# Building the first expert block's token list on chip while routing, gathering its rows in the projection's stage, and issuing that stage's last stores from ScalarE

## The chip, the core and the metric

The kernel runs on one core of a Trainium2 chip. A core has five engines with programs of their own: TensorE (PE, the matrix products), VectorE (DVE), ScalarE (ACT), GpSimd (POOL) and SyncE (SP, which here only issues transfers). They share an on-chip memory of 128 partitions and wait for each other by semaphores. The metric is the device time of one execution in microseconds, compared by the median of several runs.

## What is computed

One layer of a decoder: an input projection, two groups of attention heads (differential, and sliding window with sinks), an output projection with residual, a router that gives each of the 2048 tokens two of 32 experts, the experts, and a last norm.

```python
def reference(x, norm1_g, w_in, ..., w_gate, w_up, w_down, final_g):
    for l in range(L):                                   # L = 1
        n1 = rms_norm(x, norm1_g[l])
        qkv = n1 @ w_in[l]                               # 2048x1024 @ 1024x2304
...
        o_diff = diff_attention(dq, dk, dv, lam, subln_g[l], lambda_init)
        o_swa = swa_sink_attention(sq, sk, sv, sinks[l])
        x = x + jnp.concatenate([o_diff, o_swa], axis=-1) @ w_out[l]
        n2 = rms_norm(x, norm2_g[l])
        x = x + hier_moe(n2, ...)
    return rms_norm(x, final_g)

def hier_moe(xn, w_rg, b_rg, w_re, b_re, w_gate, w_up, w_down):
...
    p_top, g_idx = lax.top_k(pg, 1)                      # one of 4 groups
    v2, i2 = lax.top_k(el_sel, TOP_K_IN_GROUP)           # 2 of the 8 experts in it
    gates = jax.nn.softmax(v2, axis=-1) * p_top
    expert_id = (g_idx * EXPERTS_PER_GROUP + i2).astype(jnp.int32)
...
    def run_block(args):
        xb, e = args
        h = jax.nn.silu(xb @ w_gate[e]) * (xb @ w_up[e]) # 1024 -> 512
        return h @ w_down[e]                             # 512 -> 1024
```

An expert gets its tokens in blocks; the order of the tokens in a block is free.

## The kernel before

The program is a row of stages, each a block at whose end all engines meet at a barrier: `projection` (0 to about 545 us), `diff_attention` (to 790), `window_attention` (to 1061), `output_projection` (to 1329), `experts` (to 2231) and `combine` (to 2277). Products that need fp32 accuracy are made of three products of high and low parts (lines 62 to 64).

**`output_projection`** walks over 16 tiles of 128 tokens. Its order is written out by hand, engine by engine, and each engine does what stands in its program in that order. For tile t:

- TensorE does the first half of `project(t)`, then `turn(t-1)` (transposing the normed rows `n2` of the tile before), the second half of `project(t)`, `turn_o(t+1)`, then `count(t-2)` (ranks of the tokens within their experts, by a triangular matrix, line 1456) and `route(t-1)` (the router's logits, line 1449). `count` waits until VectorE has done the first step of the `place` before it.
- VectorE does `residual(t)` (h = projection + x, line 1142), `low_o(t+1)`, `normalize(t)` (n2, line 1150), `sub_norm(t+2)` (onorm, four instructions, line 1158), `low_swa(t+2)`, for tiles 1 to 8 the low part of an early weight piece (`low_w`, line 1176), then `choose(t-1)` (group and experts, 16 small instructions, lines 1185 to 1212) and `place(t-2)` (lines 1220 to 1242). `place` works out `dest`, the slot of each of a token's two choices, and `pair`, what is put there: the token's number and its gate. After the last tile `block_table` works out from the counts where each expert's blocks start and end.
- ScalarE squares `o_raw` and `h`, copies the high parts and the turned tiles, and does the exponentials of the gates.
- GpSimd takes the roots and scatters the pairs of tile t-3 into `slots_scratch` in HBM (line 1386, two indirect transfers a tile). Its program ends with a wait for all scatters.
- SyncE waits for `h` of tile t, stores it (line 1532), and only then issues the loads `swaT` and `o_raw` for tile t+2 (lines 1495, 1497), stores `n2` (line 1538) and loads x for tile t+2. At the last tile it first issues six weight loads of 1 MB each for the experts (`FIRST_LOADS`), then the last stores of `h` and `n2`, and waits for all stores.

In HBM, slot d = LISTED * p + b is place p of block b, where `LISTED` is 512, so that the first block of expert 0 holds the slots 0, 512, 1024 and so on. The slots were filled before with the number of an empty token.

**`experts`** goes over 32 experts in 47 blocks of 128 slots. GpSimd loads all slots back (line 1730), copies from them the 128 token numbers of the first block (`fetch`, line 1706) and gathers their rows of `n2` from HBM into `x` (line 1710); for later blocks it does so one block ahead. TensorE meanwhile runs 40 warming transposes (`spin`, line 56), then `turn_x(0)` (line 1836), 16 more of them, and then the products of the block (24 each for gate, up and down). ScalarE and VectorE split each tile and weight into high and low parts.

Of the kernel before, what the change touches and what calls it, by code (L numbers as in the profile page):

```python
# [7 lines left out]
F32 = mybir.dt.float32  # L8
# [1001 lines left out]
def output_projection(nc, sem, x, o_d, mix_d, wo_hi, wo_lo, wo_raw, wo_split, subln_g, norm2_g, w_rg, b_rg, w_re, b_re,  # L1010
                      ident, power, tables_d, n2_d, acc_d, slots_d, starts, ends, w_d, wg, wu,
                      hi_ready, lo_ready, next_raw, raw_in):
# [9 lines left out]
    with ExitStack() as ctx:  # L1022
# [28 lines left out]
        tri_f = sb("tri_f", [P, P])  # L1051
        consts = sb("consts5", [P, 3, E])
# [39 lines left out]
        spare = proj[:, 0, 1, 0:P]  # L1092
        count_ps = proj[0:E, 1, 1, 0:1]
# [39 lines left out]
        PLACE = 9  # L1133
        PLACED = TILES * PLACE

        with nc.Block() as block:
            @block.vector
            def _(dve):
# [105 lines left out]

                def block_table():
# [7 lines left out]
                    dve.wait_ge(counted, TILES + 2)  # L1253
                    dve.tensor_copy(start_row[:, :], start_ps).then_inc(place_step, 1)
# [14 lines left out]
                for t in range(TILES):  # L1269
# [4 lines left out]
                    if t == 0:  # L1274
                        dve.wait_ge(table_in, 32)
                        dve.tensor_copy(tri[:, :], tri_f[:, :])
                        dve.memset(ones[:, :], 1.0)
                        dve.memset(before[:, :, :], 0.0)
# [13 lines left out]
                    if t >= 2:  # L1292
                        place(t - 2, s)
                place(LAST - 1, 1 - LAST % 2)
                choose(LAST, LAST % 2)
                place(LAST, LAST % 2)
                block_table()

            @block.scalar
            def _(act):  # L1300
# [46 lines left out]
                for t in range(TILES):  # L1347
# [23 lines left out]
            @block.gpsimd  # L1371
            def _(pool):

                def sub_root(t, s):
                    pool.wait_ge(oss_ready, t * DK + DK)
                    pool.tensor_tensor(ovar[:, s, :], oss[:, s, :], power[:, 1:2].to_broadcast([P, DK]), ALU.add)\
                        .then_inc(ovar_ready, 1)
                    pool.wait_ge(ovar_ready, t + 1)
                    pool.tensor_tensor(orstd[:, s, :], ovar[:, s, :], power[:, 0:1].to_broadcast([P, DK]), ALU.pow)\
                        .then_inc(orstd_ready, 1)  # L1380

                def scatter(t):
                    pool.wait_ge(place_step, (t + 1) * PLACE)
                    pool.wait_ge(placed, 1)
                    for k in range(TOPK):
                        pool.indirect_dma_start(slots_d, bass.IndirectOffsetOnAxis(ap=dest[:, t, k:k + 1], axis=0),
                                                pair[:, t, k, :], None).then_inc(scattered, 16)

                sub_root(0, 0)
                sub_root(1, 1)  # L1390
                pool.wait_ge(tables_ready, 1)
                for k in range(TOPK):
                    ins = pool.tensor_copy(pair[:, :, k, 0].bitcast(I32), tok_i[:, :])
                ins.then_inc(placed, 1)
                for t in range(TILES):
                    s = t % 2
                    pool.wait_ge(ss_ready, t + 1)
                    pool.tensor_tensor(var[:, s:s + 1], ss[:, s:s + 1], power[:, 1:2], ALU.add).then_inc(var_ready, 1)
                    pool.wait_ge(var_ready, t + 1)
                    pool.tensor_tensor(rstd[:, s:s + 1], var[:, s:s + 1], power[:, 0:1], ALU.pow)\  # L1400
                        .then_inc(rstd_ready, 1)
                    if t + 2 < TILES:
                        sub_root(t + 2, s)
                    if t >= 3:
                        scatter(t - 3)
                for t in range(LAST - 2, TILES):
                    scatter(t)
# [666 lines left out]
```

## Time and profile before

| | |
|---|---|
| median of 3 runs | 2275.84 us (2271.41 to 2279.14) |
| the profiled execution | 2278.96 us, of which span 2277.1 us |
| busy over the span | TensorE 2086.3 us (92%), VectorE 1315.0 (58%), ScalarE 1116.1 (49%), GpSimd 514.0 (23%) |
| 1061 to 1329.5 us (output projection) | TensorE 243.8 of 268.5 us, VectorE 145.4 |
| 1329.5 to 2231 us (experts) | TensorE 876.2 of 901.5 us, VectorE 568.3 |
| mean granted clock of TensorE | 0.96 |

Busy time is the time in which an engine had an instruction under way. Waits between engines say more about what sets the pace: a view of them names, for each idle stretch, the instruction that ended it. Times in the rows below are from the start of the span; "SPq" and "POOLq" are the issues of transfers.

### The profile page before, as it was taken

What the parts mean: (1) busy time and instruction counts of PE and PEld (TensorE: products, weight loads), DVE (VectorE), ACT (ScalarE), POOL (GpSimd) and SP (SyncE); (2) the same over time, 40 slices, a digit from 0 to 9 for tenths busy, and PEclk for the clock granted to TensorE, in tenths of its full rate; (3) what the DMA queues carried; (4) which work ended last, traced back from release to release, by engine and by line L of the source; (5) the groups of instructions that cost most, each with busy time, mean ns of one, the idle gap of its engine ahead of it and who ended that gap; (6) DMA issues with size and microseconds to landing.
All of it is one profiled execution on the core that took longest, in us unless ns stands there. A gap on an engine that the chain in (4) does not pass through costs nothing. (4 is left out here: it accounts for less than half of the span.)

```text
span 2277.1 us, 39542 instructions
## 1 busy us (share of the span) xinstructions
PE 2086.3 (92%) x12823; PEld 1775.3 (78%) x12824; DVE 1315.0 (58%) x2425; ACT 1116.1 (49%) x2395; POOL 514.0 (23%) x624
## 2 busy tenths in 40 slices
PE   6999999979999994998999969999999999999990
PEld 5888888857777773997888858788888888888880
DVE  5333333348888881663555549656666648666533
ACT  4111111138778881663342337556656547666443
POOL 1111111114443434100132221111121111111114
PEclk9999999979999997998999979999999999999995
DMA  7333333252312108332554369978888979998828
GB/s 209 95 99 103 99 94 94 83 156 82 89 56 84 58 12 193 90 93 84 176 185 140 124 228 360 362 213 280 286 276 287 297 217 329 314 322 256 271 46 313
DMA packets 299719, 407.46 MB, mean 179 GB/s; under 512 B 17249, under 2 KB 211553, under 8 KB 299617
## 3 DMA queue, kind: packets, MB, share of 16 engines
q1 hardware_dynamic: 279952, 349.76, 46.1%
q0 software_dynamic: 16176, 55.09, 10.3%
q10 hardware_dynamic: 3504, 1.51, 0.3%
q8 instruction: 47, 0.77, 0.1%
q14 instruction: 40, 0.32, 0.1%
HBM read 314.01 MB, written 92.83 MB: 179 GB/s over the span
## 5 line engine op out<-in xcount | busy, mean ns | idle before, releaser
L62 PE MATMUL proj<-w_in_lo,n1T_hi 128*128 128x512 f32 (+1 forms) x640 | 245.8, 384 | 13.1 <-DVE w_in_lo L260 13.1
L63 PE MATMUL proj<-w_in_hi,n1T_lo 128*128 128x512 f32 (+1 forms) x640 | 240.3, 375 | 0.0
L64 PE MATMUL proj<-w_in_hi,n1T_hi 128*128 128x512 f32 (+1 forms) x640 | 240.0, 375 | 0.0
L534 ACT ACTIVATE prob<-score,nmax 128x512 f32<-128x512 f32 (+3 forms) x344 | 207.3, 612 | 37.0 <-DVE nmax L620 33.4
L62 PE MATMUL u_ps<-wu_lo,xT_hi 128*128 128x256 f32 x752 | 209.8, 279 | 0.0
L64 PE MATMUL u_ps<-wu_hi,xT_hi 128*128 128x256 f32 x752 | 209.7, 279 | 0.0
L63 PE MATMUL u_ps<-wu_hi,xT_lo 128*128 128x256 f32 x752 | 209.6, 279 | 0.0
L1789 DVE TENSOR_TENSOR wg_lo<-raw_pieces,wg_hi 128x1024 fp32r<-128x1024 f32 x124 | 149.0, 1221 | 91.8 <-ACT wg_hi L1761 90.0
L573 POOL TENSOR_SCALAR prob<-prob,scale,lam 128x512 f32<-128x512 f32 (+3 forms) x172 | 147.3, 867 | 229.5 <-DVE scale L636 212.9
L620 DVE TENSOR_REDUCE nmax<-score 128x2 f32<-128x1024 f32 (+3 forms) x172 | 171.3, 996 | 16.3 <-PE score L664 9.0
L62 PE MATMUL y_ps<-wd_lo,hT_hi 128*128 128x512 f32 x376 | 154.6, 411 | 5.2 <-DVE hT_lo L1800 4.5
L682 PE MATMUL o_ps<-v_sb,aT 128*128 128x128 f32 x1088 | 153.3, 279 | 5.6 <-ACT o_diff L561 4.3
L1789 DVE TENSOR_TENSOR wd_lo<-raw_pieces,wd_hi 128x1024 fp32r<-128x1024 f32 x128 | 148.3, 1219 | 13.4 <-ACT wd_hi L1781 10.8
L62 PEld LDWEIGHTS proj<-w_in_lo,n1T_hi 128*128 128x128 f32 x640 | 121.8, 190 | 36.6 <-DVE w_in_lo L260 9.4
L63 PE MATMUL y_ps<-wd_hi,hT_lo 128*128 128x512 f32 x376 | 149.8, 398 | 0.0
L64 PE MATMUL y_ps<-wd_hi,hT_hi 128*128 128x512 f32 x376 | 149.6, 398 | 0.0
L62 PE MATMUL g_ps<-wg_lo,xT_hi 128*128 128x512 f32 x376 | 149.0, 396 | 0.0
L63 PE MATMUL g_ps<-wg_hi,xT_lo 128*128 128x512 f32 x376 | 148.7, 395 | 0.0
L64 PE MATMUL g_ps<-wg_hi,xT_hi 128*128 128x512 f32 x376 | 148.7, 395 | 0.0
L1717 POOL DMA_INDIRECT acc_scratch<-y,own x48 | 84.6, 1763 | 282.2 <-issue 271.0
L682 PEld LDWEIGHTS o_ps<-v_sb,aT 128*128 128x128 f32 x1088 | 136.6, 193 | 11.2 <-ACT o_diff L561 10.8
L63 PEld LDWEIGHTS u_ps<-wu_hi,xT_lo 128*128 128x128 f32 x752 | 142.8, 190 | 2.1
(244 smaller groups left out, 5022.0 us busy)
## 6 DMA issues: line engine op xcount, KB each, us to landing
raw_pieces<-in_w_down SPq DMA_DIRECT2D x64, 1024.0 KB, 10.1
raw_pieces<-in_w_gate SPq DMA_DIRECT2D x62, 1024.0 KB, 9.6
raw_pieces<-in_w_up SPq DMA_DIRECT2D x62, 1024.0 KB, 10.3
qk_scratch<-qkT SPq DMA_DIRECT2D x96, 256.0 KB, 2.3
x_sb<-in_x SPq DMA_DIRECT2D x16, 512.0 KB, 4.2
h<-in_x SPq DMA_DIRECT2D x16, 512.0 KB, 5.5
acc_scratch<-h SPq DMA_DIRECT2D x16, 512.0 KB, 3.0
n_scratch<-n SPq DMA_DIRECT2D x16, 512.0 KB, 4.6
```

What stands on the lines that cost most here:

```text
L62: pe.matmul(out, hi, w_lo, start=first, stop=False)
L63: pe.matmul(out, lo, w_hi, start=False, stop=False)
L64: return pe.matmul(out, hi, w_hi, start=False, stop=last)
L534: act.activation(prob[:, n % RING, c, 0:w], score[:, n % BUFS, c, 0:w], ACT.Exp, bias=nmax[:, c, n:n + 1], accum_out=part[:, c, n:n + 1]). ...
L573: pool.tensor_scalar(prob[:, u % RING, 1, 0:w], prob[:, u % RING, 1, 0:w], scale[:, 1, u:u + 1], lam[:, 5:6], ALU.mult, ALU.mult).then_inc ...
L620: dve.tensor_reduce(nmax[:, :, n:n + 1], score[:, n % BUFS, :, 0:w], AX.X, ALU.max, negate=True).then_inc(max_ready, 1)
L682: mm = pe.matmul(o_ps[:, :], aT[:, u % 2, b * P:(b + 1) * P], v[:, h, j // P + b, :], start=(u == FIRST[m] and b == 0), stop=(u == LAST[m] ...
L1717: pool.indirect_dma_start(acc_d, bass.IndirectOffsetOnAxis(ap=own[:, 0:1].bitcast(I32), axis=0), y[:, :], None, compute_op=ALU.add).then_i ...
L1789: dve.tensor_tensor(piece(LO, k), raw_piece(raw, k), piece(HI, k), ALU.subtract)\
```

## The change

During routing, VectorE writes after each `place` also the list of the tokens of expert 0's first block. The new step `enlist(t)` compares the slots 0, 512, 1024 ... (`row0`, a constant table laid out along the free axis) with the two destinations of each token of the tile, multiplies by the token's number, and adds the result to `listed` (128x128, f32). After the last tile TensorE sums `listed` over the partitions by a product with a column of ones, VectorE writes that as `fetch`, and GpSimd gathers the rows into `x` still in this stage, after the stores of `n2` have landed and before it waits for its scatters. In `experts` the first gather goes away; `x` and `fetch` are now allocated outside of it. The last stores of `h` and `n2` are issued by ScalarE and no longer by SyncE behind its six weight loads.

```diff
@@ output_projection, @block.vector
+                def enlist(t):
+                    base = t * PLACE + 9
+                    dve.wait_ge(place_step, t * PLACE + 6)
+                    dve.tensor_copy(dest_f[:, :], dest[:, t, :]).then_inc(place_step, 1)
+                    dve.wait_ge(place_step, base + 1)
+                    for k in range(TOPK):
+                        dve.scalar_tensor_tensor(out=hit[:, k, :], in0=row0[:, :], scalar=dest_f[:, k:k + 1],
+                                                 in1=consts[:, 2, t:t + 1].to_broadcast([P, P]),
+                                                 op0=ALU.is_equal, op1=ALU.mult).then_inc(place_step, 1)
+                    for k in range(TOPK):
+                        dve.wait_ge(place_step, base + 3 + k)
+                        dve.tensor_tensor(listed[:, :], listed[:, :], hit[:, k, :], ALU.add).then_inc(place_step, 1)
+                    dve.wait_ge(place_step, base + 5)
...
-        PLACE = 9
+        PLACE = 14
...
                     dve.wait_ge(counted, TILES + 2)
+                    dve.tensor_scalar(fetch[:, :], listed_ps, 0.0, None, ALU.add).then_inc(fetch_ready, 1)
+                    dve.wait_ge(counted, TILES + 3)
                     dve.tensor_copy(start_row[:, :], start_ps).then_inc(place_step, 1)
...
                     if t >= 2:
                         place(t - 2, s)
+                        enlist(t - 2)
                 place(LAST - 1, 1 - LAST % 2)
+                enlist(LAST - 1)
                 choose(LAST, LAST % 2)
                 place(LAST, LAST % 2)
+                enlist(LAST)
                 block_table()
@@ @block.scalar
                     if t >= 2:
                         gate_exps(t - 2, s)
+                    if t == LAST:
+                        act.dma_start(acc_d[t * P:(t + 1) * P, :], h[:, s, :]).then_inc(h_stored[s], 16)
+                act.wait_ge(n2_ready, TILES)
+                act.dma_start(n2_d[LAST * P:TILES * P, :], n2[:, LAST % 2, :]).then_inc(stored[LAST % 2], 16)
                 turned_n2(LAST, LAST % 2)
@@ @block.tensor
+                pe.wait_ge(place_step, PLACED)
+                pe.matmul(listed_ps, listed[:, :], ones_f[:, 0:1], start=True, stop=True).then_inc(counted, 1)
@@ @block.gpsimd
                 for t in range(LAST - 2, TILES):
                     scatter(t)
+                for s in range(2):
+                    pool.wait_ge(stored[s], 8 * TILES)
+                pool.wait_ge(fetch_ready, 1)
+                pool.indirect_dma_start(x_first[:, :], None, n2_d,
+                                        bass.IndirectOffsetOnAxis(ap=fetch[:, :], axis=0)).then_inc(x_first_in, 16)
                 pool.wait_ge(scattered, 16 * TOPK * TILES)
@@ @block.sync
+                sp.dma_start(row0[:, :], tables_d[2, :, :]).then_inc(table_in, 16)
...
                             load_pair(sp, w_d, raw, raw_in, e, j)
+                        break
                     sp.wait_ge(h_ready, t + 1)
@@ experts, @block.gpsimd
                 pool.wait_ge(own_free, 32)
-                gather(0, 0)
                 pool.sem_inc(own_ready, 1)
@@ build / constants
+                    raw.append(held.enter_context(nc.sbuf_tensor("x6", [P, D], F32, side="right")))
...
-    tables = [r[:, None] < r[None, :], values]
+    tables = [r[:, None] < r[None, :], values, np.broadcast_to(r * LISTED, (P, P))]
```

GpSimd's program block also stands further down in the file, with no change of its own order but the gather.

VectorE in the middle of the output projection, at the end of a `place` and the start of the next tile, before (`h` is the residual add):

```order
L1234 SCALAR_TENSOR_TENSOR dest<-block,place 128x2 [waits p5_place_step]
L1237 SCALAR_TENSOR_TENSOR den<-vexp,gsum 128x1 [waits p5_gate_exp]
L1240 RECIPROCAL pair<-den 128x1 [waits p5_place_step]
L1242 TENSOR_TENSOR pair<-pair,vexp 128x1 [waits p5_place_step]
L1142 TENSOR_TENSOR h<-proj,h 128x1024 [waits p4_proj_ready,p4_x_in0]
L1170 TENSOR_TENSOR mixT_lo<-oT_ps,mixT_hi 128x512 [waits p4_o_high]
```

The same place on VectorE in the changed kernel:

```order
L1240 SCALAR_TENSOR_TENSOR dest<-block,place 128x2 [waits p5_place_step]
L1243 SCALAR_TENSOR_TENSOR den<-vexp,gsum 128x1 [waits p5_gate_exp]
L1246 RECIPROCAL pair<-den 128x1 [waits p5_place_step]
L1248 TENSOR_TENSOR pair<-pair,vexp 128x1 [waits p5_place_step]
L1254 CAST dest_f<-dest 128x2 [waits p5_place_step]
L1257 SCALAR_TENSOR_TENSOR hit<-row,dest_f,consts 128x128 [waits p5_place_step]
L1257 SCALAR_TENSOR_TENSOR hit<-row,dest_f,consts 128x128
L1262 TENSOR_TENSOR listed<-listed,hit 128x128 [waits p5_place_step] x2
L1148 TENSOR_TENSOR h<-proj,h 128x1024 [waits p4_proj_ready,p4_x_in1,p5_place_step]
```

Five instructions, four of them 128 elements wide, now stand between `pair` and the next `h`, and `h` waits for the last of them.

GpSimd at the end of the output projection and the start of the experts, before (the two branches are the end of one stage's program and the barrier):

```order
L1386 DMA slots_scratch<-pair,dest 65536x2
L1136 UNCONDITIONAL_BRANCH [waits p5_scattered]
L1699 UNCONDITIONAL_BRANCH [waits barrier_Pool_Activation_PE_DVE_SP_gather]
L1730 DMA slots<-slots_scratch 128x1024
L1732 DMA own<-in_empty 128x2
L1733 MEMSET y 128x1024
L1706 COPY fetch<-slots 128x1 [waits p6_own_free]
L1710 DMA x<-n_scratch,fetch 128x1024 [waits p6_x_turned,p6_fetch_ready]
```

The same place on GpSimd in the changed kernel:

```order
L1500 DMA slots_scratch<-pair,dest 65536x2
L1525 DMA x<-n_scratch,fetch 128x1024 [waits p6_fetch_ready,p4_stored1,p4_stored0]
L1142 UNCONDITIONAL_BRANCH [waits p5_scattered]
L1735 UNCONDITIONAL_BRANCH [waits barrier_Pool_Activation_PE_DVE_SP_gather]
L1766 DMA slots<-slots_scratch 128x1024
L1768 DMA own<-in_empty 128x2
L1769 MEMSET y 128x1024
```

The gather has moved from behind the barrier and the load of the slots to a place ahead of the wait for the scatters.

ScalarE at the last tile of the output projection in the changed kernel (before, the two transfers were SyncE's, behind its six weight loads, and the rest stood here as it does now):

```order
L1385 ACTIVATE sq,ss<-h 128x1024 [waits p4_ss_ready,p4_n2_ready,p4_h_ready]
L1364 ACTIVATE gexp,gsum<-lg,ngmax 128x4 [waits p5_gate_exp,p5_place_step,p5_choose_step]
L1366 ACTIVATE vexp<-top 128x1
L1395 DMA acc_scratch<-h 128x1024
L1397 DMA n_scratch<-n 128x1024 [waits p4_n2_ready]
L1356 COPY n2T<-n2t_ps 128x1024 [waits p4_n2_turned]
```

The two stores now stand ahead of the copy of the turned last tile.

## Rows read from the trace of the kernel before

**Rows 1.** Who waited for whom, 1090 to 1304 us: total us, times, longest.

```profile
ACT osq L1308 <- DMA o_raw<-o_scratch: 49.4, 13, 5.3
...
PE small_ps L1456 <- DVE home L1224: 6.0, 5, 2.4
...
DVE h L1142 <- PE proj L64: 2.6, 3, 1.8
```

**Rows 2.** VectorE in time: start, us, line, operation [idle before, releaser].

```profile
1169.30 1.22 DVE L1142 TENSOR_TENSOR h<-proj,h 128x1024 f32<-128x1024 f32 x1
...
1230.18 1.23 DVE L1142 TENSOR_TENSOR h<-proj,h 128x1024 f32<-128x1024 f32 x1
...
1238.89 1.14 DVE L1158 SCALAR_TENSOR_TENSOR onorm<-o_raw,orstd,subln_out 128x128 f32<-128x128 f32 x4 [4.00 <-POOL orstd L1379]
...
1244.67 1.23 DVE L1142 TENSOR_TENSOR h<-proj,h 128x1024 f32<-128x1024 f32 x1
...
1275.64 1.22 DVE L1142 TENSOR_TENSOR h<-proj,h 128x1024 f32<-128x1024 f32 x1 [0.46 <-PE proj L64]
...
1290.11 1.22 DVE L1142 TENSOR_TENSOR h<-proj,h 128x1024 f32<-128x1024 f32 x1
...
1304.58 1.22 DVE L1142 TENSOR_TENSOR h<-proj,h 128x1024 f32<-128x1024 f32 x1 [5.57 <-PE proj L64]
```

**Rows 3.** VectorE's instructions by form, 1060 to 1322 us: busy, mean ns, idle before.

```profile
L1142 DVE TENSOR_TENSOR h<-proj,h 128x1024 f32<-128x1024 f32 x16 | 19.6, 1224 | 12.7 <-PE proj L64 12.6
...
L1158 DVE SCALAR_TENSOR_TENSOR onorm<-o_raw,orstd,subln_out 128x128 f32<-128x128 f32 x64 | 18.2, 347 | 60.1 <-POOL orstd L1379 60.1
...
L1221 DVE TENSOR_TENSOR prod<-hot,small_ps 128x64 f32<-128x64 f32 x15 | 3.2, 214 | 0.0
```

**Rows 4.** TensorE in time; one stretch (PE, PEld, DVE, ACT, POOL, clock, DMA share, GB/s).

```profile
1168.27 0.18 PE L1456 MATMUL small_ps<-both,tri 128*128 128x32 bf16 x1 [0.90 <-DVE home L1224]
...
1177.36 1.03 PE L1443 MATMUL n2t_ps<-ident,n 128*128 128x128 f32 x8
...
1290.28 0.18 PE L1456 MATMUL small_ps<-both,tri 128*128 128x32 bf16 x1
...
1297.82 1.03 PE L1443 MATMUL n2t_ps<-ident,n 128*128 128x128 f32 x8
...
1169.00:1185.00 16.00, 16.00 (x80) 13.35 (x80) 9.91 (x37) 5.88 (x17) 5.24 (x6) 0.89 0.50 165
```

**Rows 5.** The stage's end in time; DMA issues (KB each, us to landing), last all.

```profile
1319.48 0.16 DVE L1242 TENSOR_TENSOR pair<-pair,vexp 128x1 f32<-128x1 f32 x1
...
1321.18 0.96 POOL L1386 DMA_INDIRECT slots_scratch<-pair,dest  x1 [0.30 <-issue]
...
1314.32 3.48 SPq L1532 DMA_DIRECT2D acc_scratch<-h  x1
...
n_scratch<-n SPq DMA_DIRECT2D x1, 512.0 KB, 8.3
...
slots_scratch<-pair,dest POOLq DMA_INDIRECT x2, 5.6
...
slots_scratch<-pair,dest POOLq DMA_INDIRECT x32, 2.6
```

**Rows 6.** The experts' start: TensorE, ScalarE, GpSimd in time; one stretch.

```profile
1329.71 6.58 PE L56 MATMUL y_ps<-ident 128*128 128x128 f32 x40 [9.42 <-PEq L1136]
...
1342.11 1.97 PE L1836 MATMUL xT_ps<-ident,x 128*128 128x128 f32 x8 [5.81 <-DMA x<-n_scratch,fetch]
...
1347.14 0.66 PE L62 MATMUL g_ps<-wg_lo,xT_hi 128*128 128x512 f32 x1
...
1344.11 1.01 ACT L1747 CAST xT_hi<-xT_ps 128x1024 fp32r<-128x1024 f32 x1 [9.45 <-PE xT_ps L1836]
...
1335.07 1.16 POOL L1710 DMA_INDIRECT x<-n_scratch,fetch  x1 [0.82 <-issue]
...
1342.10:1344.00 1.90, 1.90 (x9) 1.90 (x10) 0.00 (x0) 0.00 (x0) 0.18 (x1) 0.50 0.15 60
```

More of the change, by code:

```diff
@@ L1011, in output_projection @@
                       ident, power, tables_d, n2_d, acc_d, slots_d, starts, ends, w_d, wg, wu,
-                      hi_ready, lo_ready, next_raw, raw_in):
+                      hi_ready, lo_ready, next_raw, raw_in, fetch, x_first_in, fetch_ready):
     LAMBDA_INIT = 0.8 - 0.6 * math.exp(-0.3 * 0)
@@ L1051, in output_projection @@
         tri_f = sb("tri_f", [P, P])
+        row0 = sb("row0", [P, P])
+        ones_f = sb("ones_f", [P, 1])
+        dest_f = sb("dest_f", [P, TOPK])
+        hit = sb("hit5", [P, TOPK, P])
+        listed = sb("listed5", [P, P])
         consts = sb("consts5", [P, 3, E])
@@ L1369, in _ @@
                 gate_exps(LAST, LAST % 2)
[L1371 to L1407, printed above, removed]
-                pool.wait_ge(scattered, 16 * TOPK * TILES)
-                pool.sem_inc(placed, 1)
             @block.tensor
@@ L1596, in experts @@
 def experts(nc, sem, n2_d, acc_d, slots_d, empty_d, w_gate, w_up, w_down, ident, passed, wg, wu, starts, ends, hi_ready,
-            lo_ready, raw, raw_in):
+            lo_ready, raw, raw_in, x, fetch, x_in, fetch_ready):
     SIGNALLED = [0, 1, 2, 4, 6, 8, 9, 10]
@@ L1616, in experts @@
         slots = sb("slots6", [P, LISTED, 2])
-        fetch = sb("fetch6", [P, 1], I32)
         own = sb("own6", [P, 2])
-        x = sb("x6", [P, D])
         xT_hi = sb("xT_hi", [P, KD, P], F32R)
@@ L2006, in build @@
                 raw = []
+                fetch = kept("fetch6", [P, 1], I32)
+                x_in, fetch_ready = sem("p6_x_in"), sem("p6_fetch_ready")
                 def next_raw():
@@ L2010, in next_raw @@
                     raw.append(held.enter_context(nc.sbuf_tensor("raw_pieces", [P, PIECES, PW], F32, side="right")))
-                    return raw[0]
+                    raw.append(held.enter_context(nc.sbuf_tensor("x6", [P, D], F32, side="right")))
+                    return raw
                 output_projection(nc, sem, x, o_d, mix_d, wo_hi, wo_lo, wo_raw, wo_split, subln_g, norm2_g,
                                   w_router_group, b_router_group, w_router_expert, b_router_expert, ident_sb, power, tables, n2_d,
-                                  acc_d, slots_d, starts, ends, (w_gate, w_up, w_down), wg, wu, hi_ready, lo_ready, next_raw, raw_in)
+                                  acc_d, slots_d, starts, ends, (w_gate, w_up, w_down), wg, wu, hi_ready, lo_ready, next_raw, raw_in,
+                                  fetch, x_in, fetch_ready)
                 experts(nc, sem, n2_d, acc_d, slots_d, empty, w_gate, w_up, w_down, ident_sb, passed, wg, wu, starts, ends,
-                        hi_ready, lo_ready, raw[0], raw_in)
+                        hi_ready, lo_ready, raw[0], raw_in, raw[1], fetch, x_in, fetch_ready)
         combine(nc, sem, acc_d, final_g, power, out)
```

45 lines of the change are left out of this document (41 added, 4 removed).

## The prediction

> **What bounds the kernel now.** I read the page first: TensorE is busy for 92% of the span (the table above), but the change touches only the output projection's stage (1061 to 1329 us) and the first block of the experts' stage, so I read those alone. Three views matter there.
>
> First, who waits in the middle of the projection's stage [rows 1]. Before `h` (the residual add of a tile) VectorE waited for TensorE's projection only 3 times, 2.6 us in all. TensorE, the other way round, waited 5 times, 6.0 us, for VectorE's `place` ahead of its `count`. And ScalarE waited 13 times, 49.4 us, for the transfer of `o_raw`. So VectorE's program, not TensorE, sets the pace of most tiles, and it does so through a closed loop: `h` of tile t done, SyncE issues the load of `o_raw` for tile t+2, ScalarE squares it, GpSimd takes the root, VectorE does `onorm` for t+2, then the split, `choose`, `place`, and only then `h` of tile t+1.
>
> Second, VectorE in order of time [rows 2]. From `h` at 1230.18 to `onorm` at 1238.89 it is 8.7 us (the loop over the transfer), from there to the next `h` at 1244.67 5.8 us without a pause. That makes 14.5 us a tile; TensorE's own work for a tile is 1290.28 to 1304.58, 14.3 us [rows 2, 4]. The two are level to within 0.2 us, and in tiles up to 9, where VectorE also splits an early weight piece (1.2 us), it is behind. Whatever is put on VectorE between `onorm` and `h` lengthens the tile.
>
> Third, the way into the experts [rows 5, 6]. The last scatter starts on GpSimd at 1321.18 and needs 5.6 us, to 1326.8; TensorE's warming transposes start 2.9 us later, at 1329.71, and take 6.6 us, to 1336.3. The gather of the first rows is issued only at 1335.07, after the slots have come back from HBM, and lands at 1342.1. TensorE stood idle 5.81 us for it, then turned `x` at a granted clock of 0.50 (the 1.2 GHz level), and the first expert product ran at 1347.14.
>
> **The change, part by part.** I write R(t) for the start of `h` of tile t; R(15) is 1304.58.
>
> *`enlist` on VectorE, 16 times.* Five instructions and a final wait, directly behind `place`. The copy of two elements is as small as `pair`, 0.16 us [rows 5]; about 0.03 us pass until what depends on it starts, so 0.19. The two `hit` have the form of `onorm` (scalar_tensor_tensor, 128x128 f32): 347 ns each; four of them took 1.14 us in the row of 1238.89, so they follow each other at (1.14 - 0.347)/3 = 0.265 us [rows 2, 3]. First to second 0.265, second to its end plus the wait 0.38. The two adds are 128x128 tensor_tensor, between 214 ns for 64 elements and 1224 ns for 1024 [rows 3]: 214 + 64 x (1010/960) = 281 ns, and 0.03 to the next, 0.31 each. Sum: 0.19 + 0.265 + 0.38 + 2 x 0.31 = 1.46 us, with the rounding of the hand-overs 1.47. Bounds: 1.25 (all four at the pitch of 0.265 without the dependence) and 1.6.
>
> The Trainium skill ("VectorE: DVE Perf Modes", section "The TRN2 errata — SBUF-src ops pay a fixed extra latency per instruction") gives two prices for such an instruction. Its table has 58 cycles of 0.96 GHz and one more per element, by which an estimate for 128 elements is 194 ns and for `enlist` some 0.85 us, which would take 7 us off the sum. Its measured formula, (N + 151)/0.96 for an fp32 tensor_tensor, gives 1224 ns at 1024 elements, which is the trace's row exactly, and 291 ns at 128. The trace sides with the second.
>
> *Where it lies on the path.* `enlist(t-2)` stands before R(t+1). For R(3) to R(14), 12 tiles, VectorE came from `place` straight into `h` or within a few tenths: 12 x 1.47 = **+17.6 us**. Off that goes the slack that VectorE had in two of them: 0.54 us before the `h` of 1275.64 (0.46 of idle time in the row, and the 0.08 by which a next instruction starts behind `pair`) and some 0.15 before 1290.11, **-0.7**. For R(15) it costs nothing: VectorE had no `onorm` left and stood 5.57 us idle before it [rows 2], which covers `enlist(12)`.
>
> *What TensorE gives back in the last tile.* TensorE's `count` waits for the first step of `place`, which always comes before `h`: at 1168.27, 1.03 us before the `h` of 1169.30 [rows 2, 4]. With `enlist` in between it will be 2.5 us before R(14). From `count` to the next `h` is 14.3 us (1290.28 to 1304.58), so R(15) follows R(14) by 11.8 us instead of 14.47, if the clock holds. It may not: behind the wait of 0.90 us ahead of 1168.27 the stretch from 1169 to 1185 has a mean granted clock of 0.89, so a part of it ran at the 1.2 GHz level, and from `count` to the next `turn` it took 9.1 us (1168.27 to 1177.36) where it took 7.5 in the last tile (1290.28 to 1297.82) [rows 4]: 1.5 us lost. The loop hides that in the middle; in the last tile it shows. I count it for one tile in two (a slow stretch removes the next wait), so **-1.9** (-2.7 to -1.2). R(15) moves by 17.6 - 0.7 - 1.9 = **+15.0 us**.
>
> *After R(15).* `enlist(13)` and `enlist(14)` stand before `choose(15)` and `place(15)`, which ran back to back: the last `pair` and with it the last scatter come 2.9 us later, at 1324.1 (times from here on as if R(15) had not moved). This is nearly covered: before, the scatter's landing took 5.6 us among 6 MB of weight loads; the median of all 32 scatters is 2.6 [rows 5], and the bytes ahead of it, which stay the same, were all in by 1326.1 (below). I take 3.5 and so 1327.6 against 1326.8, **+0.8** (-0.1 to +2.9). `enlist(15)`, the 128x1 product and `fetch` end near 1325, beside the scatter; the gather's issue (1.16 us) ends near 1326.5, before the landing.
>
> *The last two stores from ScalarE's queue.* Before, SyncE issued the store of `h` behind six loads at 1314.32 and needed 3.48 us for that alone, so that `n2` went out at 1317.8 and landed 8.3 us later, at 1326.1 [rows 5]. Now ScalarE issues it at about 1309.9, when `n2` is there. Even with the 8.3 us of before it is down by 1318.2, well ahead of `fetch`. ScalarE's next work, the copy of the turned `n2`, waits for TensorE until some 0.6 us later, which hides a short issue. If each of its issues stalls like SyncE's 3.48 us, that copy comes some 4 us late, and `choose(15)`, which needs its product, has its own delay of 2.9 us as cover: about 1 us left. Taken: 0. The `row0` load and two memsets fall into waits at the start: 0.
>
> *The gather, 9 us earlier.* Issued at 1325.4, it lands by 1332.4 even with the 7.0 us of before. The warming transposes run 1330.5 to 1337.1 at the full clock at their end, and `turn_x` follows at once: 1.03 us, as for the eight like it at 1297.82, instead of 1.97 at half clock [rows 4, 6]. ScalarE's copy (1.01) starts at 1338.2, VectorE's subtraction (1.22, the size of `h`) ends at 1340.5, the first product is at about **1340.6 instead of 1347.14**. So with the +0.8 already in it: **-6.5 us** (-7.4 to -4.4). The experts then run as before, TensorE-bound, and the shift stays to the end.
>
> **Sum.** +15.0 - 6.5 = **+8.5 us**. The profiled execution took 2278.96 us (span 2277.1 and 1.9 around it), so 2287.5 in its terms; it lies 3.1 us above the median of 2275.84, and against that the forecast is **2284.3 us**, slower by 0.37%. The term's own bounds (12 x 0.2 for `enlist`, 0.8 for the last tile, 2 for the landing) make it 2280 to 2289.
>
> **Rivals.** *(a) The loop absorbs `enlist`.* If VectorE's stretch from `onorm` to `h` were not binding, only the gain would be left: 2275.8 - 6.5 = 2269.3, faster by 0.3%. It takes 1.5 us of slack before `h`, and the trace shows 0.5, 0.15 and nothing in ten other tiles. Chance 0.07.
> *(b) `enlist` costs less.* If its wide instructions are no dearer than the small ones of `place` (`pair`, 0.16 and 0.03 to the next), it is 5 x 0.19 = 0.95 us: 12 x 0.95 - 0.7 - 1.8 = 8.9 for R(15), less a gain of 7.4 with the scatter 1.9 instead of 2.9 us late: +1.5, 2277.3, no change that can be measured. Between faster and slower decides 0.83 us an `enlist`. The rows of 347 and 1224 ns, where the size counts, speak against it. Chance 0.1. The table of 58 cycles in the Trainium skill ("VectorE: DVE Perf Modes", the section named above) would bring this case about.
> *(c) The gain is partly lost.* If the last scatter still needs 5.6 us, or ScalarE's store issues stall, the experts start 2 to 3 us later: +11.5, 2287; with both and a transfer that lands late in one tile (each such costs some 1.5 us) 2290. For it speaks that the gather now shares the queue. Chance 0.15.
> *(d) TensorE's clock.* Each tile now leaves TensorE 1.3 to 2.7 us idle. If it drops to 1.2 GHz in every tile, 14.5 + 1.5 = 16.0 us against the loop's 15.9 costs little, but the turn and routing of the last tile would run at half speed, some 3 us: 2287.5. Chance 0.1.
> *(e) The forecast*, 0.58.
>
> **How the numbers follow.** The likeliest case gives 2284.3. To hold 8 in 10, the range takes in (b), (c) and (d): 2277 to 2291; it leaves out (a) and the ends of the others. A measurement of this kernel can tell about 0.3%, 6.8 us. Of the forecast's 0.58 some two thirds lie above 2282.7; with (c) and (d) that makes slower 0.65, within 0.3% 0.27, faster 0.08.
>
> **What would show it.** In the changed kernel's trace: `hit` at about 347 ns and `h` of a middle tile 15.9 us after the one before it instead of 14.5; the early tiles near 17; no idle time of VectorE before `h`; TensorE idle 1 us or more before `count` in about every second tile; the last `h` 15 us later than 1304.58; the gather landed before the experts begin, no idle time before `turn_x`, and 36 us from the last `h` to the first expert product instead of 42.6. I would be wrong if the middle tiles keep 14.5 us, or if the product still waits for `x`.

## The result and the profile after

| | before | after |
|---|---|---|
| median | 2275.84 us (5 runs, 2271.41 to 2279.14) | 2285.48 us (5 runs, 2284.99 to 2288.42) |
| profiled execution | 2278.96 us (span 2277.1) | 2284.99 us (span 2283.1) |
| mean granted clock | 0.96 | 0.957 |

The ratio is 1.0047, with a 95% interval of 1.0032 to 1.0062: slower by 7 to 14 us, with 2284.3 us forecast.

I read the traces with the same three questions as before. First, who waits in the projection's stage (total us, times, longest; 1090 to 1320 us of the kernel after):

```profile
DVE onorm L1164 <- POOL orstd L1493: 53.4, 13, 5.9
ACT osq L1335 <- DMA o_raw<-o_scratch: 48.2, 13, 5.4
...
PE small_ps L1447 <- DVE home L1230: 13.7, 6, 4.0
```

```profile
DVE h L1148 <- PE proj L64: 2.3, 2, 1.9
```

ScalarE's wait for the transfer is what it was in [rows 1]. VectorE waits for the projection a little less than before. TensorE's wait for `place` ahead of `count` has grown from 6.0 to 13.7 us: TensorE now has the slack, and VectorE's loop sets every tile.

VectorE in order of time, around `enlist(9)` and in the last two tiles, in the kernel after:

```profile
1227.85 1.22 DVE L1148 TENSOR_TENSOR h<-proj,h 128x1024 f32<-128x1024 f32 x1
...
1236.42 1.14 DVE L1164 SCALAR_TENSOR_TENSOR onorm<-o_raw,orstd,subln_out 128x128 f32<-128x128 f32 x4 [3.86 <-POOL orstd L1493]
...
1242.11 0.16 DVE L1248 TENSOR_TENSOR pair<-pair,vexp 128x1 f32<-128x1 f32 x1
1242.19 0.16 DVE L1254 CAST dest_f<-dest 128x2 f32<-128x2 int32 x1
1242.39 0.61 DVE L1257 SCALAR_TENSOR_TENSOR hit<-row,dest_f,consts 128x128 f32<-128x128 f32 x2
1243.04 0.62 DVE L1262 TENSOR_TENSOR listed<-listed,hit 128x128 f32<-128x128 f32 x2
1243.69 1.22 DVE L1148 TENSOR_TENSOR h<-proj,h 128x1024 f32<-128x1024 f32 x1
...
1308.59 1.23 DVE L1148 TENSOR_TENSOR h<-proj,h 128x1024 f32<-128x1024 f32 x1
...
1321.89 1.22 DVE L1148 TENSOR_TENSOR h<-proj,h 128x1024 f32<-128x1024 f32 x1 [2.99 <-PE proj L64]
```

From `dest_f` to the next `h` is 1.50 us, and `h` follows `pair` by 1.58 instead of 0.08. From `h` at 1227.85 to `onorm` it is 8.57 us, as before (8.7), and from `onorm` to `h` 7.27 instead of 5.8. Together that makes 15.84 us a tile. The waits of VectorE for the root ahead of `onorm`, 53.4 us in the view above, are still there (54.1 in the kernel before): `enlist` stands beside these waits, not in them.

VectorE's new instructions by form, 1100 to 1320 us (busy, mean ns, idle before):

```profile
L1257 DVE SCALAR_TENSOR_TENSOR hit<-row,dest_f,consts 128x128 f32<-128x128 f32 x26 | 8.0, 349 | 0.5
L1262 DVE TENSOR_TENSOR listed<-listed,hit 128x128 f32<-128x128 f32 x26 | 7.6, 292 | 0.9
```

TensorE in the last tile, and that stretch (PE, PEld, DVE, ACT, POOL, clock, DMA share, GB/s):

```profile
1306.06 0.18 PE L1447 MATMUL small_ps<-both,tri 128*128 128x32 bf16 x1 [1.23 <-DVE home L1230]
...
1315.14 1.03 PE L1434 MATMUL n2t_ps<-ident,n 128*128 128x128 f32 x8
```

```profile
1306.00:1322.00 16.00, 15.94 (x80) 13.30 (x80) 10.49 (x46) 2.63 (x6) 3.81 (x4) 0.89 0.17 67
```

`count` waited 1.23 us, the clock of the stretch is 0.89, and the `turn` comes 9.1 us after `count`: a slow stretch like that of [rows 4], now in the last tile, which before ran it in 7.5.

The stage's end and the experts' start in the kernel after: VectorE, GpSimd, ScalarE's queue, then TensorE:

```profile
1339.78 0.16 DVE L1248 TENSOR_TENSOR pair<-pair,vexp 128x1 f32<-128x1 f32 x1
...
1342.00 0.16 DVE L1274 TENSOR_SCALAR fetch<-proj 128x1 int32<-128x1 f32 x1
```

```profile
1341.54 0.96 POOL L1500 DMA_INDIRECT slots_scratch<-pair,dest  x1 [0.30 <-issue]
1342.98 1.00 POOL L1525 DMA_INDIRECT x<-n_scratch,fetch  x1 [0.47 <-issue]
1349.33 0.59 POOL L1766 DMA_DIRECT2D slots<-slots_scratch  x1 [5.35 <-POOLq L1142]
```

```profile
1323.32 0.36 ACTq L1395 DMA_DIRECT2D acc_scratch<-h  x1
...
1326.63 0.35 ACTq L1397 DMA_DIRECT2D n_scratch<-n  x1
```

```profile
1354.96 1.04 PE L1871 MATMUL xT_ps<-ident,x 128*128 128x128 f32 x8
1355.83 1.91 PE L56 MATMUL y_ps<-ident 128*128 128x128 f32 x16
1358.45 0.50 PE L62 MATMUL g_ps<-wg_lo,xT_hi 128*128 128x512 f32 x1 [0.70 <-DVE xT_lo L1829]
```

ScalarE's issues take 0.36 us each; SyncE's of the last `h`, behind its six weight loads, took 3.48. `turn_x` no longer waits and runs at full clock. The first expert product stands 36.56 us behind the last `h` (42.56 before), although GpSimd enters the experts' stage 27.44 us behind it (its load of `slots`), where it did so 25.25 us behind it before.

So the changed part, from `h` of tile 2 to the first expert product, took 251.24 us instead of 242.06, **+9.18 us**, against a difference of the medians of 9.6. The two spans differ by 6.0 us only, because the parts around it, whose code is the same, happened to differ: `h` of tile 2 began 2.13 us later, and the experts took 5.3 us less. The traces of the experiments below show that both vary that much between kernels with the same code there. That is why I compare the kernels over this part from here on.

### The profile page after: what moved, and what is told of

Same layout as the page of the kernel before. It is cut to its first block and busy times, and to the rows that moved or that the text cites. A ratio compares the mean times of both kernels' runs of the same rounds, so it can differ in the third digit from the quotient of the medians.

```text
span 2283.1 us, 39631 instructions
## 1 busy us (share of the span) xinstructions
PE 2085.6 (91%) x12825; PEld 1773.4 (78%) x12826; DVE 1338.8 (59%) x2508; ACT 1116.7 (49%) x2395; POOL 539.5 (24%) x623
## 5 line engine op out<-in xcount | busy, mean ns | idle before, releaser
L1753 POOL DMA_INDIRECT acc_scratch<-y,own x48 | 103.9, 2165 | 254.3 <-issue 243.1
L1824 DVE TENSOR_TENSOR wu_lo<-raw_pieces,wu_hi 128x1024 fp32r<-128x1024 f32 x124 | 143.3, 1219 | 0.0
```

What stands on the lines that cost most here:

```text
L1753: pool.indirect_dma_start(acc_d, bass.IndirectOffsetOnAxis(ap=own[:, 0:1].bitcast(I32), axis=0), y[:, :], None, compute_op=ALU.add).then_i ...
L1824: dve.tensor_tensor(piece(LO, k), raw_piece(raw, k), piece(HI, k), ALU.subtract)\
```

## The experiments

Eight kernels, in two jobs, each job with its own runs of the kernel before (medians 2276.12 and 2275.77 us). All kernels, in us; R is the start of `h`, "first product" that of the experts, "entry" GpSimd's load of `slots`, "last issue" its last indirect transfer of the projection's stage:

| kernel | median | ratio to before, 95% | R(2) to R(15) | last issue after R(15) | entry after R(15) | first product after R(15) | R(2) to first product |
|---|---|---|---|---|---|---|---|
| before | 2275.84 | | 199.50 | 16.60 | 25.25 | 42.56 | 242.06 |
| after | 2285.48 | 1.0047 (1.0032 to 1.0062) | 214.68 | 21.09 | 27.44 | 36.56 | 251.24 |
| enlist_only | 2290.43 | 1.0074 (1.0050 to 1.0098) | 216.77 | 19.65 | 26.12 | 44.85 | 261.62 |
| no_enlist | 2265.56 | 0.9965 (0.9951 to 0.9979) | 200.81 | 17.86 | 25.70 | 35.62 | 236.43 |
| moved | 2268.03 | 0.9972 (0.9955 to 0.9989) | 198.11 | 21.15 | 27.58 | 36.93 | 235.04 |
| after_early | 2258.25 | 0.9934 (0.9916 to 0.9953) | 187.20 | 21.09 | 27.60 | 37.44 | 224.64 |
| stores_only | 2272.45 | 0.9988 (0.9971 to 1.0006) | 198.85 | 16.60 | 25.62 | 42.61 | 241.46 |
| before_early | 2264.32 | 0.9958 (0.9938 to 0.9978) | 188.12 | 16.60 | 25.11 | 41.78 | 229.90 |
| moved_early | 2258.24 | 0.9915 (0.9886 to 0.9943) | 187.20 | 21.13 | 27.49 | 36.96 | 224.16 |
| double | 2304.93 | 1.0126 (1.0094 to 1.0158) | 230.50 | 25.36 | 31.59 | 40.86 | 271.36 |

The columns behind the ratio come from one trace of each kernel. The last column's distance from before's agrees with that of the medians to within 2.7 us in seven of the nine kernels; for enlist_only and no_enlist the two differ by 5.3 and 4.9 us.

### The list alone

```diff
@@ on the kernel before, @block.vector
                         place(t - 2, s)
+                        enlist(t - 2)
                 place(LAST - 1, 1 - LAST % 2)
+                enlist(LAST - 1)
                 choose(LAST, LAST % 2)
                 place(LAST, LAST % 2)
+                enlist(LAST)
...
+                    dve.tensor_scalar(fetch_l[:, :], listed_ps, 0.0, None, ALU.add)
```

> The kernel before, with the change's listing work alone: enlist in VectorE's stream, the list's product on TensorE and its copy on VectorE, but nothing reads the list; the last stores stay on SyncE's queue and the rows of expert 0's first block are gathered in the experts' stage, as before. Theory (the five instructions of 1.49 us stand in the closed loop h, o_raw transfer, square, root, onorm, choose, place, next h): from the h of tile 2 to that of tile 15, 214.7 us as in the kernel after and not 199.5; the stage ends later by that and by some 1 to 3 us more behind the last h, none of the early gather's 6.0 us comes back, so about 15 to 18 us over the kernel before, 2291 to 2294 us. Rival 1 (the added time came from the transfers or queues that were moved, not from the list): within 2 us of the kernel before. Behind the last h: if the early gather is what holds the stage's end in the kernel after, TensorE's next phase starts some 25 to 26 us behind the last h; if the later scatter alone does, 27.3 us.

Measured: slower, ratio 1.0074, that is 11 to 22 us (15 to 18 expected; the medians are 14.3 apart). The tiles took 216.77 us, so the list alone brings the whole loss, and nothing that was moved is needed for it. That is 2.1 us more than in the kernel after, of which 1.56 us are in the last tile: there R(15) follows R(14) by 14.86 us instead of 13.30, with a clock of 0.80 instead of 0.89 in the stretch:

```profile
1305.00:1322.20 17.20, 17.20 (x77) 14.23 (x76) 10.17 (x45) 2.63 (x6) 3.81 (x4) 0.80 0.16 62
```

So what TensorE gives back in the last tile hangs on how long its clock stays low. `count` stands 2.5 us ahead of R(14) in both kernels; from there to R(15) it is 14.30 us in a trace at full clock (stores_only), 15.83 in the kernel after and 17.38 here. Against the 14.47 us between R(14) and R(15) before, that gives 1.2 us back in the kernel after and nothing here, where it costs 0.4. Behind the last `h`, GpSimd entered the experts at 26.12 us, between the kernels before (25.25) and after (27.44) and near the 25 to 26 expected if the early gather is what holds the stage's end, and issued its gather only 6.4 us later, so that the first product came at 44.85:

```profile
1341.77 0.95 POOL L1497 DMA_INDIRECT slots_scratch<-pair,dest  x1 [0.30 <-issue]
1348.24 0.59 POOL L1757 DMA_DIRECT2D slots<-slots_scratch  x1 [5.51 <-POOLq L1143]
```

So of the 2.19 us by which the kernel after enters late, the late scatter makes 0.9 and the gather 1.3. VectorE, whose table of the blocks is the last work before the barrier on the other engines, ends 20.9 us behind the last `h` in both kernels, so it isn't what makes them differ. The landings say what the end of the stage waits for. The last scatter, in the kernel before (issued at 1321.18) and here (1341.77), takes this long from issue to landing:

```profile
slots_scratch<-pair,dest POOLq DMA_INDIRECT x1, 5.2
```

```profile
slots_scratch<-pair,dest POOLq DMA_INDIRECT x1, 3.0
```

GpSimd enters the experts about 3.5 us behind that landing in both. For the early gather three traces have the landing: 5.7 us in no_enlist, 4.3 in moved, and in after_early

```profile
x<-n_scratch,fetch POOLq DMA_INDIRECT x1, 4.4
```

There the entry comes 2.2, 2.1 and 2.1 us behind the gather's landing. So the stage also waits for the gather to land, although nothing in it reads `x`. (The trace of the kernel after lacks the landing; its times fit.)

### The move alone, without the list

```diff
@@ on the kernel after
-                        enlist(t - 2)
...
-                enlist(LAST - 1)
...
-                enlist(LAST)
...
-                    dve.tensor_scalar(fetch[:, :], listed_ps, 0.0, None, ALU.add).then_inc(fetch_ready, 1)
+                    dve.tensor_tensor(fetch[:, :], listed_ps, consts[:, 2, 0:1], ALU.add).then_inc(fetch_ready, 1)
```

> The kernel after without the listing work in the tiles (conversion, two hits, two additions); the list that the early gather reads is simply the tokens 0 to 127, so the first block of expert 0 is computed for the wrong tokens; everything else is the kernel after. Theory: the tiles take 199.5 us from the h of tile 2 to that of tile 15, as before, and the first product of the experts comes 6 us less behind the last h than before's 42.6 us, about 36 us or, with the last scatter 3 us earlier too, 33 to 36 us: 6 to 9 us under the kernel before, 2266 to 2270 us. Rival (the early gather and the stores on ScalarE's queue are worth nothing by themselves, the gain in the profile is from elsewhere): within 2 us of the kernel before.

Measured: faster, ratio 0.9965, 5 to 11 us. The tiles took 200.81 us (199.50 before), and the first product stood 35.62 us behind the last `h`. The early gather, with the stores that let it go early, is worth 6.9 us there. The price of the list is the distance to the kernel after: 19.9 us by the medians, 14.8 by one trace each in the changed part. I can't place the 5.1 us between the two; single executions of this kernel lie between 2258.85 and 2272.75 us.

### The list's place in the stream

```diff
@@ on the kernel after, @block.vector
                     normalize(t, s)
+                    if 3 <= t < LAST:
+                        enlist(t - 3)
                     if t + 2 < TILES:
                         sub_norm(t + 2, s)
...
-                        enlist(t - 2)
+                    if t == LAST - 1:
+                        enlist(t - 2)
...
+                for t in (LAST - 2, LAST - 1, LAST):
+                    enlist(t)
                 block_table()
```

> The kernel after with enlist of tile t-3 put between VectorE's two normalizations of tile t, where it waits for GpSimd's root in any case, under a count of its own; the last three lists come behind place of tile 15. Theory (the position in the stream decides, not VectorE's total work): the 1.49 us fall into a wait, the tiles take 199.5 to 202 us from the h of tile 2 to that of tile 15, the last scatter's issue comes 3 us earlier behind the last h, the list some 1.5 us later; 2268 to 2274 us. Rival (VectorE's total work sets the tile, or the added writes slow what shares memory with them): the tiles stay at 214.7 us and the time at 2284 to 2287 us.

Measured: faster than before, ratio 0.9972, with the same list and the same work on VectorE. The tiles took 198.11 us. VectorE in a middle tile of this kernel (the copy `dest_f` left out):

```profile
1221.59 1.28 DVE L1158 SCALAR_TENSOR_TENSOR n<-h,rstd,g_bc 128x1024 f32<-128x1024 f32 x1 [1.61 <-issue]
...
1222.98 0.61 DVE L1259 SCALAR_TENSOR_TENSOR hit<-row,dest_f,consts 128x128 f32<-128x128 f32 x2
1223.63 0.62 DVE L1264 TENSOR_TENSOR listed<-listed,hit 128x128 f32<-128x128 f32 x2
...
1226.66 1.19 DVE L1166 SCALAR_TENSOR_TENSOR onorm<-o_raw,orstd,subln_out 128x128 f32<-128x128 f32 x4 [2.41 <-POOL orstd L1498]
```

The wait ahead of `onorm` was 3.86 us in the kernel after; now it is 2.41, and the 1.5 us between are the list. This run separates place from amount: VectorE was not too busy; the list had stood in a part of its stream that the loop runs through. Had VectorE's total work set the tile, the list would have cost the same here.

### Opening the loop

```diff
@@ on the kernel after, SyncE
+                    if t + 2 < TILES:
+                        sp.wait_ge(onorm_ready, t + 1)
+                        sp.wait_ge(swa_split, t + 1)
+                        load(t + 2, s)
...
-                    if t + 2 < TILES:
-                        load(t + 2, s)
```

> The kernel after, with SyncE's load of tile t+2 of o_raw and swaT issued as soon as the buffers are read (onorm and low part of the own tile done), instead of behind the store of h. This opens the loop that runs through h, the transfer, the square, the root and onorm. Theory (that loop, with its transfer, sets 15.8 to 17.0 us per tile): the tile falls to what the busiest engine needs, about 14.4 us (TensorE), 0.8 to 1.7 us less for each of 13 tiles, 13 to 27 us less in the stage; 2258 to 2272 us. Rival (VectorE's own work sets the tile now): within 3 us of the kernel after.

Measured: faster, ratio 0.9934, and 27.2 us under the kernel after although the list stays where it was. From tile 2 on each tile took 14.40 us, to the hundredth. In the 180 us from 1110 to 1290 TensorE was busy all the time, at full clock (first the kernel after, then this one):

```profile
1110.00:1290.00 180.00, 167.52 (x836) 140.03 (x835) 110.71 (x411) 58.60 (x179) 49.72 (x63) 0.93 0.44 145
```

```profile
1110.00:1290.00 180.00, 180.00 (x980) 152.07 (x979) 129.49 (x479) 67.48 (x204) 68.45 (x74) 1.00 0.48 161
```

ScalarE's wait for `o_raw` is gone from the view of waits, and VectorE waits for TensorE (1110 to 1297 us):

```profile
DVE onorm L1164 <- POOL orstd L1493: 14.3, 12, 1.2
DVE h L1148 <- PE proj L64: 9.6, 8, 3.0
```

That shows the loop: what set 15.8 us and more was not any engine's work but the chain behind the load that waited for `h`.

### The same edit on the kernel before

```diff
@@ on the kernel before, SyncE
+                    if t + 2 < TILES:
+                        sp.wait_ge(onorm_ready, t + 1)
+                        sp.wait_ge(swa_split, t + 1)
+                        load(t + 2, s)
...
-                    if t + 2 < TILES:
-                        load(t + 2, s)
```

> The kernel before with SyncE's load of tile t+2 of o_raw and swaT issued as soon as the buffers are read, not behind the store of h. Theory (the loop through h and the transfer sets the tile in before too, only less tightly): 14.4 us per tile as with the same edit on the kernel after (187.2 us from the h of tile 2 to that of tile 15, not 199.5), 12 us less: 2263 to 2265 us. Rival (only the longer loop of the kernel after is worth opening): within 3 us of the kernel before. With 187.2 us in both, enlist costs nothing in the tiles where TensorE sets the pace.

Measured: ratio 0.9958; 188.12 us in the tiles, 11.4 less, and the median 11.5 us lower. So the loop bound before too, by about 0.9 us a tile. With it open, VectorE stood 27.6 us idle for the projection ahead of `h` (1104 to 1291 us), against 9.6 us with the list: the 18.0 us between are about 12 lists of 1.5, now paid for from idle time. The list is free in the tiles here. The tiles were 0.07 us longer than with it (14.47 against 14.40 us, so 188.12 and not the 187.2 expected); I did not find out why.

```profile
DVE h L1142 <- PE proj L64: 27.6, 13, 3.1
```

### Both edits

```diff
@@ on the kernel after
                     normalize(t, s)
+                    if 3 <= t < LAST:
+                        enlist(t - 3)
...
+                        sp.wait_ge(onorm_ready, t + 1)
+                        sp.wait_ge(swa_split, t + 1)
+                        load(t + 2, s)
```

> Both edits on the kernel after: enlist between VectorE's two normalizations, and the early load of tile t+2. Theory: TensorE sets 14.4 us per tile, 187.2 us from the h of tile 2 to that of tile 15, as with the early load alone, so moving enlist adds nothing there; behind the last h the first product of the experts comes at 36.9 us (as with enlist moved alone) and not 37.4: 2256 to 2259 us, 5 to 7 us under the kernel before with the same early load, since only that lacks the early gather. Rival (VectorE is close behind TensorE, and what stands in its stream matters still): 3 us or more apart from the early load alone.

Measured: median 2258.24 us, ratio 0.9915. The tiles took 187.20 us, the same as with the early load alone, and the first product stood 36.96 us behind the last `h`, against 37.44 with the early load alone. The two medians are equal. Moving the list adds nothing once TensorE sets the pace. Against the kernel before with the same early load it is 6.1 us less by the medians. By the traces it is 5.7 us less in the changed part: 4.8 behind the last `h`, where the early gather works, and 0.9 in the tiles. This and the early load alone are the fastest kernels here, and I can't tell them apart.

### The stores alone

```diff
@@ on the kernel before, ScalarE and SyncE: the stores of h and n2 of tile 15
+                    if t == LAST:
+                        act.dma_start(acc_d[t * P:(t + 1) * P, :], h[:, s, :]).then_inc(h_stored[s], 16)
+                act.wait_ge(n2_ready, TILES)
+                act.dma_start(n2_d[LAST * P:TILES * P, :], n2[:, LAST % 2, :]).then_inc(stored[LAST % 2], 16)
...
+                        break
```

> The kernel before with the last stores of h and n2 on ScalarE's queue, nothing else. Theory (these stores stand behind nothing that waits for them on either queue): the tiles 199.5 us from the h of tile 2 to that of tile 15, the first product of the experts 42 to 43 us behind the last h, within 2 us of the kernel before. Rival (part of the early gather's gain is these stores, which no longer stand behind SyncE's weight loads): the stage ends 1 to 3 us earlier behind the last h, 2273 to 2275 us.

Measured: ratio 0.9988 with an interval that includes 1. In the trace the first product stands 42.61 us behind the last `h` (42.56 before) and the entry at 25.62 (25.25). The stores by themselves bring nothing behind the last `h`. The median is 3.3 us under before's, more than the 2 us expected, but nothing in the stage's end of the trace accounts for it. What the stores are there for is to let the early gather read `n2` in time; no run has the early gather without them.

### The list twice

```diff
@@ on the kernel after, in enlist: the same five instructions again, into another list
+                        dve.tensor_tensor(listed2[:, :], listed2[:, :], hit[:, k, :], ALU.add).then_inc(place_step, 1)
```

> The kernel after with enlist twice in each tile, the second into a list that nothing reads: ten instructions of 3.0 us where the kernel after has five of 1.49. Theory (closed loop): each tile from 2 to 14 longer by another 1.49 us less what slack a tile has, 18 to 20 us more from the h of tile 2 to that of tile 15 (233 to 234.5 us), the last scatter and the gather each 3 us later behind the last h, and the stage's end 6.4 us behind the gather's issue, so 3 us later too: 21 to 23 us over the kernel after, 2305 to 2309 us. Rival (the cost of the first enlist is a step, a missed turn of TensorE or a clock that fell, and not proportional): under 12 us over the kernel after.

Measured: 2304.93 us, ratio 1.0126, 19.5 us over the kernel after, a little under what I expected (21 to 23). From R(2) to R(15) it was 15.8 us more, not 18 to 20. Ten of the twelve tiles grew by about 1.6 us each (15.6 in all), and two did not: the tiles that took 19.0 and 17.4 us in the kernel after took 18.8 and 17.8. These two are the ones in which VectorE waited longest for the root in the kernel after:

```profile
1134.63 0.61 DVE L1164 SCALAR_TENSOR_TENSOR onorm<-o_raw,orstd,subln_out 128x128 f32<-128x128 f32 x2 [5.86 <-POOL orstd L1493]
...
1269.52 0.61 DVE L1164 SCALAR_TENSOR_TENSOR onorm<-o_raw,orstd,subln_out 128x128 f32<-128x128 f32 x2 [5.41 <-POOL orstd L1493]
```

With the list twice the first of these waits is an ordinary one:

```profile
1134.42 1.14 DVE L1165 SCALAR_TENSOR_TENSOR onorm<-o_raw,orstd,subln_out 128x128 f32<-128x128 f32 x4 [4.18 <-POOL orstd L1505]
```

The second is 4.27 us. So the two tiles did not absorb the second list: from `onorm` to the next `h` they grew by 1.49 us like the others, and the long wait ahead of `onorm` did not come again (ScalarE's longest wait for `o_raw` fell from 5.4 to 3.9 us). Behind the last `h` the gather was issued 4.3 us later than in the kernel after, and not 3, since three lists stand ahead of it there. The rival of a single step is out: the price is close to proportional.

## Why the prediction was right, step by step

- **The closed loop: right.** The tiles kept the 8.6 us over the transfer and got the list on top. The tile of 15.84 us was forecast at 15.9, the early ones at "near 17" and were 16.9 to 17.0, but for one of 18.95 us with a long wait for the root. Moving the list out of that part of the stream and opening the loop each took the loss away, by different means.
- **The price of `enlist`: right**, 1.50 us where I took 1.47. `hit` took 349 ns (347 taken from `onorm`), `listed` 292 (281 interpolated). The Trainium skill's measured formula for a tensor_tensor ("VectorE: DVE Perf Modes", section "The TRN2 errata — SBUF-src ops pay a fixed extra latency per instruction") gives 291 ns, which the trace confirms; by its table of 58 cycles and one per element it would be 194 ns, which the trace refutes for this form. Rival (b) falls with it.
- **Twelve tiles: right.** R(2) to R(14) grew by 16.35 us, where 17.6 - 0.7 = 16.9 was forecast. From `onorm` to the next `h` the tiles grew by 17.3 us in all, which is twelve lists of 1.50 less the 0.7 of slack; from `h` to `onorm` they were 0.9 shorter.
- **What TensorE gives back: right in kind.** -1.17 us instead of -1.9. That was a mean of two cases, and the slow one came (1.2 was its bound). The size is less sure than the kind: R(15) followed R(14) by 14.47 us in the kernel before and by 13.57 in stores_only, whose code up to there is the same, because TensorE's `count` stood 0.17 us behind R(14) in one trace and 0.73 ahead of it in the other. R(15) moved by 15.18 us relative to R(2), with 15.0 forecast.
- **The experts' start: one wait left out.** The late scatter was forecast to cost +0.8 us there, and with the list alone it cost 0.9. (The last scatter of before took 5.2 us to land; the 5.6 of the forecast is the median of two.) The kernel after was +2.19 late. What failed is that the stage was taken to end with its scatters, while the gather, issued 1.44 us behind the last of them, could still be on its way (the forecast let it land at 1332.4 and the warming start at 1330.5). In the three traces that show its landing, the stage ends 2.1 to 2.2 us behind it: that is the other 1.3 us.
- **The first product: near.** 36.56 us behind the last `h`, where 36.0 was forecast, so -6.0 and not -6.5. The late start was partly made up, since the warming transposes took 5.75 us up to `turn_x` and not 6.6.
- **ScalarE's stores at nothing: right**, 0.36 us each, and nothing behind the last `h` in the trace of the stores alone. Of rival (c) neither half came: the stores' issues did not stall, and the last scatter took 3.0 us with the list alone, not 5.6. The later entry has the other reason that (c) names in passing, that the gather shares the queue.
- **"The experts then run as before": not visible in one trace.** They took 924.65 us from the first product on instead of 929.96. That isn't the change: kernels with the same experts' code and no early gather took 924.9 (the list alone), 924.1 (before with the early load) and 929.2 (the stores alone).
- **Absorption, rival (a): out.** It comes true only with the list moved, or the loop open.
- **TensorE's clock, rival (d): present and small in this kernel.** 0.93 instead of 0.97 from 1110 to 1290 us; it costs where no loop hides it, in the last tile, about 1.5 us from `count` to R(15). The 3 us that (d) gives for the last tile came with the list alone, at a clock of 0.80.

The sum was +8.5; the changed part measured +9.18 in its trace and the medians +9.6, with an interval of 7 to 14 us. The mechanism was right and is shown by the runs. That the number came out within 1.2 us is partly luck: the later entry (+1.4 us over its forecast) was made up in part by the faster warming (-0.8), the smaller give-back of TensorE (+0.7) by the tiles (-0.5), and the last tile alone varies by about 1 us between traces of the same code.

## What to carry to other kernels

Ask of an added instruction not how busy its engine is but which stretch of its stream closes a loop: here the same 1.5 us cost 1.4 us a tile behind `place` and nothing in the wait ahead of `onorm`. Where several engines seem level, look for a transfer whose issue waits for something that it does not need; issuing it when its buffer is free gained 11.5 us on the kernel before, more than the early gather, and 27.2 us on the kernel after. And when the parts around the change vary by several microseconds between runs, compare the traces between two fixed points around the change and not by their spans.

## What the runs showed of the hardware

- **The end of the stage.** It follows the landing of the last indirect transfer: GpSimd's first transfer of the next stage came about 3.5 us behind the last scatter's landing in two kernels without the early gather, and 2.1 to 2.2 us behind the gather's in three with it. Why the two differ by 1.4 us is open. Counted from the issue it is 6.23 to 6.51 us in the six kernels whose last indirect issue started later than 19 us behind the last `h`, and more in the four where it started at 16.6 or 17.9 (entry at 25.1 to 25.7): in the two of these whose landing the traces have, the transfer itself took longer, 5.2 and 5.7 us. The weight loads were still running then, up to 21 or 22 us behind the last `h`; that they slow it is not shown by itself.
- **Early parts drift.** With nearly the same code ahead of it, `h` of tile 2 began between 1099.73 and 1111.60 us in the ten traces. The experts' part took 923.7 to 930.0 us.
- **The clock after a short wait.** TensorE waited 1.2 to 1.3 us ahead of `count` in the last tile of the kernel after and with the list alone, and the stretches of 16 and 17 us around and behind it had a mean granted clock of 0.89 and 0.80. With the loop open it had no wait and a clock of 1.00 over the 180 us from 1110.
